# A two-layer decoder trunk in float32: raw x through the first projections with the rms factor applied at evictions, the router by channel halves, angles later, a layer's first group by terms

## The chip, the core and the metric

The kernel is one program on one core of a Trainium2 chip. The metric is the time of one execution on the device in microseconds (us), lower is better; a kernel's time is the median of its runs.

Engines, as the profile names them: PE (TensorE: matmuls and transposes, PEld its weight loads), DVE (VectorE), ACT (ScalarE), POOL (GpSimd) and SP (SyncE, which here issues nearly all DMAs). Engines run on their own and meet at semaphores.

## The reference

```python
def rms_norm(x, g):
    return x * lax.rsqrt(jnp.mean(x * x, axis=-1, keepdims=True) + EPS) * g

for l in range(DEPTH):                        # 2 layers, x is (1, 256, 1024) f32
    h = rms_norm(x, norm_mix_g[l])
    proj = h @ w_in[l]                        # u va | q k v | index q, k, weights | conv b c x | 3 gates
    ya = gelu(u) * spatial(layer_norm(gelu(va)))         # causal 128x128 mix per channel group
    yb = attention(q, k, v) over the 64 best causal keys of a small indexer, partial rotary
    yc = cb * conv3(cc * cx)
    x = x + (sigmoid(g0) * (ya @ w_proj_a) + sigmoid(g1) * (yb @ w_proj_b) + sigmoid(g2) * (yc @ w_proj_c)) @ w_out
    h = rms_norm(x, norm_ffn_g[l])            # best of 4 groups, then the 2 best of its 8 experts
    x = x + sum over the 2 experts e of weight_e * (silu(h @ w_gate[e]) * (h @ w_up[e])) @ w_down[e]
return rms_norm(x, norm_final_g)
```

All data is float32, the 256 tokens are two tiles of 128 (index t), the 1024 channels eight chunks of 128.

## The kernel before, in words

Each engine has a program of its own, written out by hand; the order of an engine's work is the order of its lines, and every wait is a semaphore. For each of the two layers:

**Mixers.** The projections run as 9 groups of 512 columns (the first, G_QI, has 324), then 6 gates, 6 branch projections and 2 halves of w_out. Each needs weights in two parts: SP loads a raw 1 MB half into one of 6 ring slots (load_mix), ACT rounds it to a high part (`high`, L740), DVE subtracts to get the low part (`low`, L944), and PE multiplies high by high, high by low and low by high into PSUM (`product`, L1392, 48 or 96 matmuls a group). A unit is the two halves of one group: unit 0 is G_QI, 1 G_Q, 2 G_K, 3 G_V, 4 G_VA, 5 G_U, 6 G_CX, 7 G_CC, 8 G_CB. G_QI to G_VA put tokens on the partitions, G_U, G_CX, G_CC and G_CB channels. Results alternate between psA and psB; a group waits until the result two before it was evicted (by ACT, or by DVE for the conv groups). The activations are split likewise into hT_high and hT_low.

**The start of a layer** (mixing_norm, in three programs): the squares of x are summed (ACT L705, DVE L959), a square root on ACT (L745) with one Newton step on DVE gives rstd, x is scaled by it (ACT L709, DVE L968), PE transposes it (L1422), ACT scales by the gain and rounds to hT_high (L696), DVE makes hT_low (L977). Between them DVE copies the layer's parameters and makes G_QI's low parts. G_QI's matmuls take all three terms of a channel chunk before the next chunk. In layer 0 DVE first works out the rotary angles (L894 to L906) and ACT their sines, and x, positions and two small tables come on SP's queue ahead of the weights, the router's weights on ACT's.

**The key selection** (DVE, L1034 to L1041): for each of the two token tiles 4 score operations and 8 rounds of MAX8 and MATCH_REPLACE8. Behind the second stand the statistics of va (L1048), then the low parts of G_CX.

**Routing**: DVE adds the w_out result to x, PE transposes x with channels strided by 8, ACT and DVE scale it by the ffn gain into hT, PE makes 16 router products, then spins (`spin`, matmuls whose result nobody reads) until DVE has the expert choice (members); rank products, a selection matrix, and the first gather follow.

**Experts**: 16 pairs of experts, each with 12 slots of 1 MB through the whole ring of 20; the last pair stands in a loop that also takes overflow blocks. SP refills a slot once its stage of the pair has been used (pair_freed).

## Time and profile before

| | us |
|---|---|
| median of 3 runs (1438.97 to 1439.96) | 1439.09 |
| the profiled execution's own time | 1437.3 |
| its span | 1435.6 |
| PE busy | 1385.5 (97%) |
| DVE busy | 559.2 (39%) |
| ACT busy | 361.2 (25%) |
| DMA moved | 490.19 MB, mean 341 GB/s |

The span runs from the first to the last instruction of the profiled execution. Times inside it are counted from its start. Layer 0's mixers take some 250 us, its routing 15, its experts 445; layer 1 begins near 716 and has the same stages. The profile's mean granted TensorE clock is 0.992 of full speed (2.4 GHz).

### The profile page before, as it was taken

To read this page: it belongs to the slowest core of one execution; us is meant where nothing else is said; L and a number is where in the kernel's file an instruction comes from. 1 tells how busy PE (TensorE), PEld (TensorE's weight loads), DVE (VectorE), ACT (ScalarE), POOL (GpSimd) and SP (SyncE) were. 2 spreads that over 40 slices of the span, in tenths; PEclk is the share of its full clock that TensorE was granted. 3 is DMA by queue.
4 is the path that set the end of the run, shared out by engine and by line. 5 is a ranking of instruction groups with operands and counts; after the bars stand their busy time and mean duration, and the time that the engine had idled before them with its cause. 6 is when DMAs were issued, how large, how long until landed. Compare 5 with 4: busy or idle time off the path is not lost.

```text
span 1435.6 us, 17698 instructions
## 1 busy us (share of the span) xinstructions
PE 1385.5 (97%) x7295; PEld 833.4 (58%) x7295; DVE 559.2 (39%) x882; ACT 361.2 (25%) x532; POOL 6.3 (0%) x36
## 2 busy tenths in 40 slices
PE   5999999999999999999889999999999999999996
PEld 5899888644444444444378988885444444444442
DVE  6686655432221221221267757355222122122213
ACT  5554442311111111111155444422111111111111
POOL 0000000000000000000000000000000000000000
PEclk9999999999999999999989999999999999999999
DMA  8655767899999999999946457578999999999995
GB/s 282 195 189 177 252 203 278 347 422 421 421 421 421 421 420 421 421 422 421 405 138 220 153 200 265 204 317 346 422 421 420 420 421 422 421 421 421 420 421 226
DMA packets 101125, 490.19 MB, mean 341 GB/s; under 512 B 8717, under 2 KB 12085, under 8 KB 51893
## 3 DMA queue, kind: packets, MB, share of 16 engines
q1 hardware_dynamic: 99940, 488.72, 85.4%
q8 instruction: 58, 0.95, 0.3%
q10 hardware_dynamic: 1104, 0.34, 0.1%
q14 instruction: 23, 0.18, 0.0%
HBM read 487.98 MB, written 1.05 MB: 341 GB/s over the span
## 4 chain that ended last, share of the span: by engine, by line
PE 89%; DVE 7%; issue 2%; ACT 1%; DMA 0%; DVEq 0%; SPq 0%; ACTq 0%
PE psB L1644 31%; PE psC L1655 16%; PE psA L1392 13%; PE psB L1392 12%; PE psA L1633 8%; PE psA L1670 3%; PE psA L1671 2%; DVE parts L944 2%; PE psD L1697 1%; DVE score_work L1039 1%; DVE top L1038 1%; ACT parts L740 1%; PE psC L1608 1%; DVE score_work L1034 0%; DMA rows<-in_conv_w_dram 0%
## 5 line engine op out<-in xcount | busy, mean ns | idle before, releaser
L1644 PE MATMUL psB<-slot,uT 128*64 128x512 f32 x2048 | 458.8, 595 | 0.0
L1644 PEld LDWEIGHTS psB<-slot,uT 128*64 128x64 f32 x2048 | 141.2, 137 | 268.4 <-issue 265.6
L1655 PE MATMUL psC<-slot,ybT_plain 128*64 128x512 f32 x1024 | 227.2, 595 | 2.8 <-ACT ybT_plain L855 2.7
L944 DVE TENSOR_TENSOR parts<-slot,parts 128x2048 fp32r<-128x2048 f32 (+1 forms) x80 | 177.4, 2248 | 70.3 <-ACT parts L740 70.0
L740 ACT ACTIVATE parts<-slot 128x2048 fp32r<-128x2048 f32 (+1 forms) x80 | 147.9, 1879 | 92.8 <-PE psA L1392 50.1
L1655 PEld LDWEIGHTS psC<-slot,ybT_plain 128*64 128x64 f32 x1024 | 70.9, 137 | 135.1 <-issue 128.2
L1268 DVE TENSOR_TENSOR x<-x,psA 128x1024 f32<-128x1024 f32 x62 | 75.7, 1221 | 186.3 <-PE psA L1671 186.3
L1392 PE MATMUL psB<-parts,hT_parts 128*128 128x512 f32 x448 | 138.9, 391 | 0.2
L1633 PEld LDWEIGHTS psA<-sel_mem,xn 128*128 128x128 f32 x1024 | 119.2, 192 | 27.0 <-issue 25.7
L839 ACT ACTIVATE rel_parts<-psC 128x512 fp32r<-128x512 f32 x62 | 37.1, 598 | 385.5 <-PE psC L1655 259.3
L1633 PE MATMUL psA<-sel_mem,xn 128*128 128x128 f32 x1024 | 127.4, 278 | 2.5 <-DVE sel_mem L1227 2.5
L1259 DVE TENSOR_TENSOR rel_parts<-psC,rel_parts 128x512 fp32r<-128x512 f32 x62 | 42.6, 688 | 222.3 <-ACT rel_parts L839 222.3
L1392 PE MATMUL psA<-parts,hT_parts 128*128 128x512 f32 (+1 forms) x384 | 115.3, 383 | 1.9 <-DVE low_mem_parts L977 1.9
L1392 PEld LDWEIGHTS psB<-parts,hT_parts 128*128 128x128 f32 x448 | 83.4, 188 | 18.5 <-DVE tmp L1151 1.0
L1280 DVE SCALAR_TENSOR_TENSOR ybT_plain<-score_work,slot_w,psB 128x512 f32<-128x512 f32 x32 | 23.9, 747 | 170.1 <-PE psB L1644 170.1
L1392 PE MATMUL psB<-parts,low_mem_parts 128*128 128x512 f32 x224 | 87.2, 389 | 0.0
L1392 PEld LDWEIGHTS psA<-parts,hT_parts 128*128 128x128 f32 x384 | 71.9, 192 | 14.8 <-issue 2.7
L1253 DVE TENSOR_TENSOR uT<-psA,g_ffn 128x512 f32<-128x512 f32 x64 | 44.3, 692 | 87.1 <-PE psA L1633 87.1
L1392 PE MATMUL psA<-parts,low_mem_parts 128*128 128x512 f32 (+1 forms) x192 | 73.1, 381 | 0.0
L855 ACT ACTIVATE ybT_plain<-psD 128x512 f32<-128x512 f32 x32 | 19.1, 597 | 165.6 <-PE psD L1697 165.6
L1670 PE MATMUL psA<-rel_parts,selT 128*128 128x512 f32 x124 | 55.5, 447 | 2.8 <-DVE rel_parts L1259 2.8
L1670 PEld LDWEIGHTS psA<-rel_parts,selT 128*128 128x128 f32 x124 | 23.2, 187 | 55.9 <-issue 48.7
(302 smaller groups left out, 1179.2 us busy)
## 6 DMA issues: line engine op xcount, KB each, us to landing
slot<-in_expert_w_gate_dram SPq DMA_DIRECT2D x128, 1024.0 KB, 21.7
slot<-in_expert_w_up_dram SPq DMA_DIRECT2D x128, 1024.0 KB, 23.2
slot<-in_expert_w_down_dram SPq DMA_DIRECT2D x128, 1024.0 KB, 24.3
slot<-in_w_in_dram SPq DMA_DIRECT2D x56, 1024.0 KB, 5.1
slot<-in_w_out_dram SPq DMA_DIRECT2D x8, 1024.0 KB, 5.1
slot<-in_w_proj_b_dram SPq DMA_DIRECT2D x4, 1024.0 KB, 5.0
slot<-in_w_proj_c_dram SPq DMA_DIRECT2D x4, 1024.0 KB, 4.9
slot<-in_w_proj_a_dram SPq DMA_DIRECT2D x4, 1024.0 KB, 5.0
```

Source lines behind the costliest of these rows:

```text
L740: sc.activation(high_and_low(i)[0], mix_slot(i), ACT.Copy).then_inc(high_act, 1)
L839: sc.activation(to[:, 0, :], psC[:, n, :], ACT.Copy).then_inc(y_act, 1)
L944: v.tensor_tensor(low_part, mix_slot(i), high_part, ALU.subtract).then_inc(low_dve, 1)
L1253: v.tensor_tensor(xT[:, 4 * b:4 * b + 4, :], psA[:, b, :].rearrange("p (c n) -> p c n", c=4), g_ffn[:, 4 * b:4 * b + 4].unsqueeze(2).to_br ...
L1259: v.tensor_tensor(to[:, 1, :], psC[:, n, :], to[:, 0, :], ALU.subtract).then_inc(y_dve, 1)
L1268: v.tensor_tensor(to, to, (psB if last and n else psA)[:, :, :], ALU.add).then_inc(x_added, 1)
L1392: ins = te.matmul(o, first, second, start=start and i == 0, stop=stop and i == len(TERMS) - 1)
L1633: ins = te.matmul(psA[:, b, (c % 4) * P:(c % 4 + 1) * P], xn[:, o:o + P], sel_plain[:, t, :], start=t == 0, stop=t == NT - 1)
L1644: ins = te.matmul(psB[j * BLK:(j + 1) * BLK, o, :], xT[:, 4 * half + c, j * BLK:(j + 1) * BLK], w[:, c, :], start=half == 0 and c == 0, st ...
L1655: ins = te.matmul(psC[j * BLK:(j + 1) * BLK, n, :], hidT[:, 2 * k + c, j * BLK:(j + 1) * BLK], w[:, c, n * 512:(n + 1) * 512], start=k == ...
L1670: te.matmul(ps[:, t, :], selT[:, t, :], y[:, 0, :], start=True, stop=False)
L1671: ins = te.matmul(ps[:, t, :], selT[:, t, :], y[:, 1, :], start=False, stop=True)
```

## The change

- **Raw x.** PE transposes x as it is, without rstd; ACT and DVE make hT_high and hT_low with the gain alone. rstd (now rstd_mix) is worked out behind them and applied where results are evicted: token-major groups and gates by ACT's scale, one instruction for each token tile (`normed`); for G_U and G_CX DVE multiplies by a row of rstd that PE makes with a ones matrix (`rstd_to_row`), for G_CX the row is squared, which covers the product with G_CC; G_CB's factor goes into its gate's product on DVE. G_U is therefore evicted by DVE, and ACT applies the gelu behind it.
- **The first group by terms.** In each half of G_QI all high by high products come first, then high by low weights, then low activations by high weights, each with its own wait; the high and low parts are made in that order.
- **Angles and sines** move behind the high and low parts of units 0 and 1. The small tables and positions go to ACT's queue, the router's loads to SP's, behind the sixth weight load; the router's weights are now laid out by chunks, so that they come in pieces of 16 and 128 bytes. Nine matmuls on ones open PE's program.
- **The router by channel halves.** x's channels are transposed without a stride; the first half of them between the two token tiles of the last w_out product; x is added by token tile. The ffn gain is multiplied into the router's weights, in `parameters`, which moves behind the low parts of unit 4. Each token tile's logits have their own signal. 15 spins instead of 14, and 4 more behind the rank products.
- **The key selection.** The low parts of G_CX are made between rounds 5 and 6 of the second selection; the statistics of va move behind the softmax's last step.

Three places, as the two kernels order them. ACT at the start of the program, before (parts are the high parts of a raw slot):

```order
L682 ACT_TABLE_LOAD
L682 ACTIVATE sin<-ang 128x32 [waits setup_link]
L683 ACTIVATE cos<-ang 128x32
L687 ACT_TABLE_LOAD
L687 ACTIVATE spare<-ones 128x1
L705 ACTIVATE xn,ss<-x 128x1024 [waits x_added,x_landed]
L745 ACTIVATE rstd<-inv 128x2 [waits inv_dve]
L740 ACTIVATE parts_81<-slot_75 128x1296 [waits staged2]
L709 ACTIVATE xn<-x,rstd 128x1024 [waits rstd_dve]
```

and in the change:

```order
L759 ACT_TABLE_LOAD [waits staged2]
L759 ACTIVATE parts_82<-slot_76 128x1296 [waits setup_done]
L703 ACTIVATE hT_parts<-psC,cols 128x256 [waits hT_ps]
...
L759 ACTIVATE parts_84<-slot_78 128x2048 [waits staged4]
L759 ACTIVATE parts_85<-slot_79 128x2048 [waits staged5]
L720 ACT_TABLE_LOAD
L720 ACTIVATE sin<-ang 128x32 [waits setup_link]
L721 ACTIVATE cos<-ang 128x32
L694 ACT_TABLE_LOAD
L694 ACTIVATE spare<-ones 128x1
L725 ACTIVATE xn,ss<-x 128x1024 [waits x_added,x_landed]
```

The weights' high parts and hT_high now stand ahead of the sines and the squares, and the program's first table load stands behind the wait for the first weights.

DVE in the second key selection, in the change:

```order
L1073 MAX top<-score_work 128x8 [waits dve_link]
L1074 MATCH_REPLACE score_work<-top,score_work 128x256 [waits dve_link]
L974 TENSOR_TENSOR parts_88<-slot_76,parts_82 128x2048 [waits dve_link,high_act]
L974 TENSOR_TENSOR parts_89<-slot_77,parts_83 128x2048 [waits high_act]
L1073 MAX top<-score_work 128x8
L1074 MATCH_REPLACE score_work<-top,score_work 128x256 [waits dve_link]
...
L1077 TENSOR_TENSOR maskb<-score_work 128x256 [waits dve_link]
L1078 SCALAR_TENSOR_TENSOR maskb<-maskb,causal 128x256 [waits dve_link]
L1084 TENSOR_TENSOR uT<-psB,rstd_row 128x1024 [waits mixed,dve_link]
```

The two low parts of G_CX stood behind the masks and four instructions of statistics; now three rounds and the masks stand behind them, and DVE's own eviction of G_U.

PE in the routing, in the change, from the last products of w_out on:

```order
L1463 MATMUL psD<-ident,x 128x128 [waits x_mixed]
L1463 MATMUL psD<-ident,x 128x128 x3
L1469 MATMUL psB<-r_w,hT 128x36 [waits routeT_act,layer_params]
L1469 MATMUL psB<-r_w,hT 128x36 x3
L1469 MATMUL psB<-r_w,hT 128x36 [waits routeT_act]
L1469 MATMUL psB<-r_w,hT 128x36 x3
L1463 MATMUL psD<-ident,x 128x128 [waits dve_out]
L1463 MATMUL psD<-ident,x 128x128
L1463 MATMUL psC<-ident,x 128x128 x2
L1469 MATMUL psB<-r_w,hT 128x36 [waits routeT_act]
```

Before, all 16 transposes stood behind the last add to x and ahead of all router products; now eight stand inside the w_out product, four behind its first token tile (x_mixed) and four behind the last add (dve_out).

The diff, cut to its core:

```diff
 sync_program:
-            with nc.allow_non_contiguous_dma(reason="256 positions"):
-                sp.dma_start(pos_i[:, :], positions.rearrange("a (t p) -> p (a t)", p=P)).then_inc(pos_landed, 16)
             for t in range(NT):
                 sp.dma_start(x[:, t, :], x_in[0, t * P:(t + 1) * P, :]).then_inc(x_landed, 16)
-            sp.dma_start(rows[0:DEPTH * KC, :], norm_mix_g.rearrange("l (c p) -> (l c) p", p=P)).then_inc(rows_landed, 16)
-            sp.dma_start(rows[DEPTH * KC:, :], conv_w.rearrange("l k (c p) -> (l k c) p", p=P)).then_inc(rows_landed, 16)
...
                     load_mix(i)
+                    if l == 0 and i == RAWS - 1:
+                        router_loads(sp)
...
-        def router_loads(act):
+        def router_loads(sp):
...
+                for l in range(DEPTH):
+                    sp.dma_start(rg_all[:, l], router_group_w.rearrange("l (c p) n -> l p c n", p=P)[l]).then_inc(router_landed, 16)
+                    sp.dma_start(re_all[:, l], router_expert_w.rearrange("l (c p) n -> l p c n", p=P)[l]).then_inc(router_landed, 16)
...
 scalar_program:
-            router_loads(act)
-            act.wait_ge(setup_link, TRIG_READY)
-
-            sc.activation(sin[:, :, :], ang[:, 0], ACT.Sin)
-            sc.activation(cos[:, :, :], ang[:, 1], ACT.Sin).then_inc(trig_act, 1)
+            act.dma_start(rows[0:DEPTH * KC, :], norm_mix_g.rearrange("l (c p) -> (l c) p", p=P)).then_inc(rows_landed, 16)
...
                 def mixing_norm():
 
+                    if l:
+                        act.wait_ge(pair_freed, start * STAGES)
+                    act.wait_ge(setup_done, 1)
+                    for i in range(2):
+                        high(unit_slots(0)[i])
+                        for b in (2 * i, 2 * i + 1):
+                            act.wait_ge(hT_ps, l * 4 + b + 1)
+                            even_bank((psC, psD)[i], b, hT_high, cols[:, l * KC:(l + 1) * KC])
+                    high(*unit_slots(1))
+                    if l == 0:
+                        act.wait_ge(setup_link, TRIG_READY)
+                        sc.activation(sin[:, :, :], ang[:, 0], ACT.Sin)
+                        sc.activation(cos[:, :, :], ang[:, 1], ACT.Sin).then_inc(trig_act, 1)
                     sqrt_table()
...
                     root_of(0)
-                    high(unit_slots(0)[0])
-                    act.wait_ge(rstd_dve, l * 2 + 1)
-                    sc.activation(xn[:, 0:D], x[:, 0, :], ACT.Copy, scale=rstd[:, 0:1]).then_inc(xn_act, 1)
-                    high(unit_slots(0)[1])
...
+                def normed(dst, n, func):
+
+                    ps = result(n)
+                    for t in range(NT):
+                        ins = sc.activation(dst[:, t, :], ps[:, t, :], func, scale=rstd_mix[:, t:t + 1])
+                    ins.then_inc(act_out, 1)
...
 vector_program:
                 def mixing_norm():
 
-                    squares(0)
-                    newton_step(l * 3 + 1, link).then_inc(rstd_dve, 1)
-                    dve.wait_ge(rstd_dve, l * 2 + 1)
-                    v.tensor_scalar(xn[:, D:2 * D], x[:, 1, :], rstd[:, 1:2], None, ALU.mult).then_inc(xn_dve, 1)
-                    parameters()
-                    dve.wait_ge(layer_params, l + 1)
-                    low(*unit_slots(0))
-
                     for b in range(4):
-                        dve.wait_ge(hT_act, l * 6 + b + 1)
+                        if b % 2 == 0:
+                            low(unit_slots(0)[b // 2])
+                        dve.wait_ge(hT_act, l * 4 + b + 1)
...
                     low(*unit_slots(1))
+                    if l == 0:
+                        angles()
+                    squares(0)
+                    newton_step(l * 3 + 1, link, rstd_mix).then_inc(rstd_dve, 1)
...
+                        if b == 1 and r == TOPK // 8 - 4:
+                            low(*unit_slots(6))
...
+                row = rstd_row[:, :].unsqueeze(1).unsqueeze(1).to_broadcast([P, 2, 2, S])
+                v.tensor_tensor(uT[:, :, :].rearrange("p (b h) s -> p b h s", b=2),
+                                result(G_U)[:, :, :].rearrange("p b (h s) -> p b h s", h=2), row, ALU.mult).then_inc(dve_out, 1)
...
 tensor_program:
+            pe.wait_ge(ones_set, 1)
+            for _ in range(9):
+                te.matmul(psC[:, 0, 0:P], ones[:, :], ones[:, :], start=True, stop=True)
...
+                    if step == G_QI:
+                        for i in range(2):
+                            use = USE[step, i]
+                            w = [part.rearrange("p (c n) -> p c n", c=4) for part in high_and_low(use)]
+                            for a, b in TERMS:
+                                for c in range(4):
+                                    k = 4 * i + c
...
+                            if part == 1 and t == 0:
+                                ins.then_inc(out_ps, 1)
+                                if half == 1:
+                                    pe.wait_ge(dve_out, l * len(on_dve) + 1 + on_dve.index(RESULT[out_of(0)]))
+                                    for u in range(NT):
+                                        route_transposes(psC[:, u, :], range(4), u)
...
+                route(1, 0).then_inc(route_ps, 1)
...
+                route(1, 1).then_inc(route_ps, 1)
+                spin(15)
```

## Rows read from the trace of the kernel before

**Rows 1.** waits of PE: waited for, us in total, times, longest us

```profile
PE psA L1392 <- DVE parts L944: 4.9, 2, 2.4
```

**Rows 2.** PE in order of time, start of layer 1: start, us, what [idle before]

```profile
721.57 1.97 PE L1422 MATMUL psA<-ident,xn 128*128 128x128 f32 x8 [5.64 <-ACT xn L709]
```

**Rows 3.** the chain that ended last: a layer's first and third group

```profile
37.28 10.93 PE psA L1392 x48
...
726.23 9.43 PE psA L1392 x48
...
747.24 10.93 PE psA L1392 x48
```

**Rows 4.** DVE and ACT in order of time, start of layer 1

```profile
717.43 1.22 DVE L959 CUSTOM_DVE_ANT_0 xn<-x 128x1024 f32<-128x1024 f32 x1
...
721.58 2.93 DVE L944 TENSOR_TENSOR parts<-slot,parts 128x1296 fp32r<-128x1296 f32 x2
...
724.43 1.65 DVE L977 SCALAR_TENSOR_TENSOR low_mem_parts<-psA,g_mix,hT_parts 128x256 fp32r<-128x256 f32 x4
...
719.21 1.27 ACT L740 ACTIVATE parts<-slot 128x1296 fp32r<-128x1296 f32 x1
...
722.78 1.63 ACT L696 ACTIVATE hT_parts<-psA,g_mix 128x256 fp32r<-128x256 f32 x4
...
726.01 3.71 ACT L740 ACTIVATE parts<-slot 128x2048 fp32r<-128x2048 f32 x2
```

**Rows 5.** DMAs of the start, us to landing; the first w_in load's; an SP issue

```profile
rg_all<-in_router_group_w_dram ACTq DMA_DIRECT2D x1, 32.0 KB, 4.0
...
g_ffn_all<-in_norm_ffn_g_dram ACTq DMA_DIRECT2D x1, 8.0 KB, 2.6
...
DMA to landing us min/median/max: 7.5/7.5/7.5
...
2.72 0.49 SPq L498 DMA_DIRECT2D rows<-in_conv_w_dram  x1
```

**Rows 6.** all engines in order of time, start of the program

```profile
3.75 0.17 DVE L894 CAST pos_f<-pos_i 128x2 f32<-128x2 int32 x1 [2.69 <-POOL causal L667]
...
6.49 1.28 ACT L687 ACT_TABLE_LOAD   x1
...
7.78 0.20 ACT L687 ACTIVATE spare<-ones 128x1 f32<-128x1 f32 x1
```

**Rows 7.** DVE, and PE's one wait, at the second key selection of layer 0

```profile
79.03 0.43 DVE L1038 MAX8 top<-score_work 128x8 f32<-128x256 f32 x1
...
83.46 1.29 DVE L1048 BATCH_NORM_STATS2 stats<-vg 128x6 f32<-128x512 f32 x2
...
85.47 4.47 DVE L944 TENSOR_TENSOR parts<-slot,parts 128x2048 fp32r<-128x2048 f32 x2
...
90.09 0.48 PE L1392 MATMUL psA<-hT_parts,parts 128*128 128x256 f32 x2 [2.44 <-DVE parts L944]
...
94.02 4.48 DVE L944 TENSOR_TENSOR parts<-slot,parts 128x2048 fp32r<-128x2048 f32 x2
```

**Rows 8.** PE and DVE, routing of layer 0

```profile
254.34 1.16 PE L1422 MATMUL psA<-ident,x 128*128 128x128 f32 x8 [1.31 <-DVE x L1172]
...
259.89 4.95 PE L1407 MATMUL psD<-before,ones 128*128 128x128 f32 x28
...
264.43 0.23 DVE L1212 TENSOR_TENSOR ycT_parts<-ycT 128x64 fp32r<-128x64 f32 x1
```

**Rows 9.** one stretch: busy us of each engine, granted clock, DMA share, GB/s

```profile
721.50:726.20 4.70, 3.68 (x16) 3.28 (x17) 4.67 (x8) 4.58 (x11) 0.00 (x0) 0.50 0.02 7
```

**Rows 10.** layer 0: two stretches; landing of the down parts issued at 677.4 and 679.5

```profile
270.00:274.20 4.20, 4.20 (x23) 1.67 (x23) 0.69 (x1) 0.00 (x0) 0.00 (x0) 1.00 0.03 14
...
290.00:600.00 310.00, 310.00 (x1588) 138.87 (x1586) 73.81 (x112) 38.65 (x99) 0.00 (x0) 1.00 1.01 421
...
DMA to landing us min/median/max: 28.6/28.8/29.1
```

More of the change, by code:

```diff
@@ L457, in build_trunk @@
         final_done = sem("final_done")
-        on_act = [n for n, step in enumerate(STEPS) if n <= G_U or is_gate(step)]
+        on_act = [n for n, step in enumerate(STEPS) if n < G_U or is_gate(step)]
         on_dve = [n for n in range(N_RESULTS) if n not in on_act]
@@ L766, in scalar_program @@
                 high(*unit_slots(3))
-                sc.activation(k_tok, result(G_K)[:, :, :], ACT.Copy).then_inc(act_out, 1)
+                normed(k_tok, G_K, ACT.Copy)
                 high(unit_slots(4)[0])
@@ L918, in variance, with newton_step @@
                 v.reciprocal(inv[:, :], var[:, :]).then_inc(inv_dve, 1)
-            def newton_step(n, step):
+            def newton_step(n, step, result=rstd):
                 dve.wait_ge(root, n)
@@ L1407, in spin, with route_transposes, route, norm_transposes @@
                         te.matmul(psD[:, 1, 0:P], ones[:, :], before[:, :], start=True, stop=True)
-                def norm_transposes(which):
-                    if which == 0:
-                        pe.wait_ge(xn_act, l * 2 + 1)
-                        pe.wait_ge(xn_dve, l + 1)
-                    else:
-                        pe.wait_ge(dve_out, (l + 1) * len(on_dve))
+                def route_transposes(bank, cs, t):
+                    for k, c in enumerate(cs):
+                        ins = te.transpose(bank[:, k * P:(k + 1) * P], x[:, t, c * P:(c + 1) * P], ident[:, :])
+                    ins.then_inc(routeT_ps, 1)
+                def route(half, t):
+                    for c in range(4 * half, 4 * half + 4):
+                        ins = te.matmul(psB[:, t, 0:N_ROUTE], hT[:, c, t * P:(t + 1) * P], r_w[:, c, :],
+                                        start=c == 0, stop=c == KC - 1)
+                    return ins
+                def norm_transposes():
+                    pe.wait_ge(x_landed, 16 * NT)
+                    pe.wait_ge(x_added, done * 2 + 1)
                     for b in range(4):
-                        ps = (psA, psB)[b // 2]
+                        ps = (psC, psD)[b // 2]
+                        if l == 0 and b == 3:
+                            pe.wait_ge(setup_done, 1)
                         for c in range(2):
@@ L1434, in group @@
                                 k = 4 * i + c
-                                if step == G_QI and k in (0, 4, 6):
-                                    pe.wait_ge(hT_dve, l * 6 + max(k // 2, 1) + 1)
                                 for t in range(NT):
@@ L1455, in index_transposes, with rstd_to_row @@
                     ins.then_inc(idxT_ps, 1)
+                def rstd_to_row():
+                    pe.wait_ge(diag_dve, l + 1)
+                    for t in range(NT):
+                        ins = te.matmul(psD[:, 1, t * P:(t + 1) * P], ones[:, :], rstd_diag[:, t, :], start=True, stop=True)
+                    ins.then_inc(row_ps, 1)
                 def index_scores():
                     pe.wait_ge(idxT_act, l + 1)
+                    pe.wait_ge(row_dve, l * 2 + 1)
                     for b, ps, nk in ((0, psD, P), (1, psC, S)):
```

237 lines of the change are left out of this document (140 added, 97 removed).

## The prediction

> **What bounds the kernel now.** I read the waits first, then the chain that ended last, then the timelines where they point. PE is busy for 97% of the span. Nearly all is matmul that the change leaves as it is, so only PE's gaps and its slow stretches can be won. Four kinds of gap are on the chain in each layer.
>
> - The start of a layer: PE sits idle for 5.64 us before its first transpose of layer 1 [rows 2], because x is summed, rooted and scaled first; G_QI starts at 726.23 and G_K at 747.24, in layer 0 G_K at 37.28 [rows 3]. PE pays twice: in 721.5 to 726.2 the granted clock is 0.50, the lower level of 1.2 GHz, after that idle time [rows 9], and G_QI takes 9.43 us.
> - Before G_CX PE waits 2.4 us for DVE's low parts, once a layer, 4.9 in all [rows 1, 7].
> - Routing: a wait of 1.31 us for x, then 16 transposes and 16 products up to 259.89, then spins that end at 264.84, as the choice does at 264.66 [rows 8].
> - The experts: DMA share 1.01 at 421 GB/s from 290 to 600, and 0.03 in 270 to 274.2, when the ring is full [rows 10]. From the first freed slot on the queue never rests, and the last down part, issued at 679.5, lands 29.1 us later, at 708.6. PE waits for no landing there, but uses this one at once: transfers and matmuls take the same 434 us. Both start with the first freed slot, so an earlier start moves both, and nothing is won or lost inside. I cost the experts and the end of the program at zero.
>
> **The change, part by part.** I measure the start of a layer at G_K's end: 48.2 and 758.2 before, both a start plus 10.93 [rows 3].
>
> *Layer 1.* x is complete at 717.43, where DVE's squares began [rows 4]. G_QI's first high part no longer waits for rstd and is made before that. Four transposes take 0.5, ACT's hT_high 0.82 a bank (1.63 for two) [rows 4]: G_QI starts at 718.8. ACT goes on: second bank 719.6, G_QI's second high part (1.27) 720.9, two banks 722.6, G_Q's two (3.71) 724.4 and 726.3 [rows 4]. DVE follows with low parts of 1.46 (2.93 for two) and 1.65 for two banks [rows 4], and 2.24 for a full one (4.48 for two) [rows 7]: G_Q's first is ready at 726.7. G_QI by terms has then run its 48 matmuls. At the full clock G_Q takes 10.9, to 737.6; the new row of rstd 0.5 and the index transposes 0.7 bring G_K's start to 738.8. Beside this stand squares, root and Newton step: DVE's low parts end at 729.0, squares 1.2 [rows 4]. Root and Newton are bounded by the 2.9 us between the end of the squares and the low parts at 721.58 [rows 4], which held more; I take 1.5. rstd is there at 731.7, G_QI evicted at 732.7, G_K's weights split in time (736.9). Nothing there is last. G_K ends at 749.7: **8.5 us** earlier.
>
> *Layer 0.* An SP issue takes 0.49 and three fewer stand ahead of the weights; the first load landed 7.5 us after its issue at 3.26 [rows 5], so now near 9.3. ACT's first table load, 1.28 [rows 6], stands behind that wait, so it is no longer hidden: 10.6. Then as above: two banks 13.5, second high part 14.8, two banks 16.4, G_Q's high parts 18.3 and 20.1, its low parts 20.5 and 22.8. G_Q runs to 31.4. Behind the low parts come the angles and sines, 2.7 (3.75 to 6.49) [rows 6], another table load 1.3, ACT's squares 1.1, root and Newton 1.5: rstd at 29.6, G_QI evicted 30.6, G_K's high part 32.5, its low part 34.7. Here the engines behind rstd are last, not PE. G_K ends at 45.6: **2.6 us** earlier. If the load comes no sooner the gain is 1.1; if the table load is hidden after all, 3.9.
>
> After each table load the next ACT operation follows at once (6.49 + 1.28, then 7.78) [rows 6], so I use 1.28. The Trainium skill (ScalarE: Activation LUTs, What ACT_TABLE_LOAD costs) puts a drain of about 1.38 us on top of each switch. By it the two loads on layer 0's path would cost 2.8 us more; the trace disagrees.
>
> *Before G_CX.* Its low parts move ahead of three rounds and the masks, 4.4 us (79.03 to 83.46), and of the statistics, 2.0 (to 85.47) [rows 7]. `parameters` moves in ahead of them at 0.9. They end 5.5 us sooner, 2.4 were needed: the wait goes, **2.4 us in each layer**. Late next would be G_CC's low parts. They ended at 98.5 [rows 7]; DVE loses the statistics there (2.0) and gains `parameters`, G_U's eviction (1.25, as other PSUM operations of this size) and the row's square (0.35), so 99.0 in the old frame. G_CX would now end at 87.7 + 11.7 = 99.4. The cover is 0.4 us.
>
> *Routing.* Behind w_out's end stood 1.31 + 5.55 us up to the last product [rows 8]. Now eight transposes (1.0) lie inside w_out, and eight more and the 16 products (4.5) need no wait for the first half of x: 5.5, so 1.3 sooner, and 1.6 for the choice because one tile's logits are handled early. But 15 spins at the old mean (4.95 for 14) [rows 8] take 5.3 and end 0.9 us behind the choice. Between 0.6 (spins last) and 1.6 (full clock) I take **1.0 in each layer**. The four spins behind the rank products fit into PE's wait for the selection matrix.
>
> *Free.* Evictions in two instructions, DVE's product with rstd for one gate, ACT's gelu behind DVE: ACT is busy 25% and DVE 39% of the span, and each has microseconds before its reader. The nine first matmuls run while x is on its way.
>
> Sum: 8.5 + 2.6 + 4.8 + 2.0 = 17.9 us. The profiled execution took 1437.3, so 1419.4 for such a run; it stood 1.8 below the median of 1439.1, so the median comes to **1421.2**.
>
> **The rivals.**
>
> *The wait moves to G_CC.* The cover of 0.4 rests on estimates of 2.5 us of added DVE work. If that comes to 2.4 us more, the gain before G_CX is given back before G_CC: 1426.0. For it: DVE has no gap in this stretch. Against: the statistics are gone. 0.12.
>
> *The clock stays low in layer 1.* PE still idles 1.5 us before the transposes and the last matmuls of a layer have gaps. With a granted 0.50, transposes take 1.9 and G_QI 2.1 more, G_Q starts some 3.6 later: 1424.8. Against: the idle time that went before the fall was 5.64 [rows 2, 9]. 0.13.
>
> *Small pieces stop SP's queue: slower.* The router's loads, some 4600 pieces of 16 to 128 bytes, now stand in SP's queue between G_K's and G_V's weights. The near rows: 256 pieces of 32 bytes landed in 2.6 us, 256 of 128 bytes in 4.0, issued 0.55 later [rows 5], so at most 1.95 for 256, and at 421 GB/s their bytes alone need 1.4 us in all. That is 1.4 to 35 us; I take 1 us for 256, 18 us. G_K's weights land near 22, G_V's then near 43 and 45, just in time for PE near 47. At 35 us PE loses 17: 1438. Above 2 us for 256 the change is slower; at 2.5, 1448. No row has pieces of 16 bytes. The Trainium skill (DMA: Bandwidth & Descriptors, Specifications) has every piece under 512 bytes pay a read-modify-write; by it this rival would come true if that doubled the rows' price. 0.08, of which 0.04 slower and 0.02 same.
>
> **The numbers.** 0.67 is left for the forecast. About 0.2% is what a measurement of this kernel can tell, 2.9 us. Faster by more 0.94, within 0.02, slower 0.04. The median forecast is 1421.2; the low end 1416.0 takes layer 0's upper bound and both full routings; the high end 1427.0 takes in the first two rivals. Beyond it lie both together and the third.
>
> **What would show it.** G_K ends near 45.6 in layer 0, and in layer 1 8.5 us nearer to the layer's last scatter; the granted clock is 1.00 in G_QI of layer 1; PE's wait for L944's successor before G_CX is gone and none stands before G_CC; the weights of G_V land before 45; the stretch from w_out's end to the gather is 2 us shorter (1.0 of it inside w_out); the DMA's busy stretch in the experts is 434 us as before. A stall on a landing in the first 60 us, or experts that stretch, would prove me wrong.

## The result and the profile after

The changed kernel takes 1418.70 us (median of 4 runs, 1418.14 to 1420.04) against 1439.15 beside it: a ratio of 0.9856, 95% interval 0.9841 to 0.9871, 20.45 us less. The forecast was 1421.2, with 17.9 us of gain. The profiled executions lie 17.3 us apart (spans 1435.6 and 1418.3). Executions of one kernel come at levels some 1.6 to 2 us apart; where two of them were traced, the difference was a short stretch at TensorE's lower clock. So places within the traces are compared here, and times only where they say enough. How far apart the medians lie depends on these levels too: beside the later experiments the kernel before had medians of 1437.48 (19 runs), 1439.18 (14, one of 5010.6 left out) and 1437.64 (7), and against 1437.6 the gain is 18.9 us.

PE is busy for 1386.7 us (98%), DVE 562.7, ACT 366.6. PE's waits, view of the waits of PE (waited for, us in total, times, longest), in answer to [rows 1]:

```profile
PE psA L1508 <- ACT hT_parts L703: 2.1, 1, 2.1
PE psD L1714 <- DVE ycT_parts L1261: 2.0, 2, 1.1
...
PE psC L1484 <- DVE x L1317: 1.5, 1, 1.5
...
PE psA L1443 <- DVE parts L974: 1.0, 1, 1.0
PE psB L1443 <- DVE tmp L1195: 0.5, 2, 0.3
PE psB L1443 <- DVE parts L974: 0.3, 2, 0.2
```

The 4.9 us before G_CX are gone. Twice 0.2 before G_CC, 2.0 before the rank products (L1714) and 0.3 in each layer at a gate product (L1195) are new. The chain that ended last, in answer to [rows 3] (the x96 rows are G_CC):

```profile
33.35 11.17 PE psA L1443 x48
...
95.61 11.75 PE psB L1443 x96
...
712.21 7.13 PE psA L1508 x48
719.34 11.14 PE psB L1443 x48
731.57 10.95 PE psA L1443 x48
...
793.58 11.74 PE psB L1443 x96
```

G_K of layer 0 ends at 44.5 (48.2 before). The start of layer 1, PE and then DVE in order of time, in answer to [rows 2, 4]:

```profile
710.24 1.09 PE L1484 MATMUL psC<-ident,x 128*128 128x128 f32 x8 [1.53 <-DVE x L1317]
711.17 1.04 PE L1484 MATMUL psD<-ident,x 128*128 128x128 f32 x8
711.96 2.65 PE L1508 MATMUL psA<-parts,hT_parts 128*128 128x324 f32 x16
```

```profile
710.22 1.51 DVE L974 TENSOR_TENSOR parts<-slot,parts 128x1296 fp32r<-128x1296 f32 x1
...
716.98 4.49 DVE L974 TENSOR_TENSOR parts<-slot,parts 128x2048 fp32r<-128x2048 f32 x2 [0.19 <-ACT parts L759]
...
723.88 0.16 DVE L956 TENSOR_TENSOR rstd_mix<-rstd,newton 128x2 f32<-128x2 f32 x1
```

x is complete at 710.19, PE multiplies from 711.96 on, and rstd, ready 13.9 us after x, is late for nothing. Two stretches of the changed kernel (busy us of each engine, granted clock, DMA share, GB/s), in answer to [rows 9]:

```profile
712.20:719.30 7.10, 7.10 (x49) 6.85 (x47) 6.67 (x11) 7.08 (x9) 0.00 (x0) 1.00 0.49 157
...
956.00:963.10 7.10, 5.95 (x39) 5.63 (x39) 2.62 (x11) 0.00 (x0) 0.00 (x0) 0.76 0.81 338
```

G_QI of layer 1 has the full clock. Layer 1's first gather has not: 5.46 us where layer 0's took 3.81. So this execution lost 1.6 us that executions with a fast gather do not lose.

The account of the profiled pair, each line the shift between the two traces:

| stretch | layer 0 | layer 1 |
|---|---|---|
| start of the layer to G_K's end | 3.7 | 8.4 |
| G_K's end to G_CC's start | 2.5 | 2.5 |
| G_CC to the last group ahead of the routing | -0.4 | -0.4 |
| from there to the gather | 1.1 | 1.1 |
| the gather at the lower clock | | -1.6 |
| gather to the end of the layer | 0.3 | 0.05 |

The sum is 17.3 (the entries are rounded). Without the slow gather it is 18.9.

### The profile page after: what moved, and what is told of

The parts are those of the page before. It is cut to its first block, busy times and chain, and to the rows that moved or that the text cites. A ratio compares the mean times of both kernels' runs of the same rounds, so it can differ in the third digit from the quotient of the medians.

```text
span 1418.3 us, 17835 instructions
## 1 busy us (share of the span) xinstructions
PE 1386.7 (98%) x7341; PEld 835.1 (59%) x7341; DVE 562.7 (40%) x892; ACT 366.6 (26%) x555; POOL 6.3 (0%) x36
## 4 chain that ended last, share of the span: by engine, by line
PE 87%; DVE 8%; ACT 3%; issue 2%; DMA 0%; DVEq 0%; SPq 0%; ACTq 0%
PE psB L1743 32%; PE psC L1754 16%; PE psB L1443 12%; PE psA L1443 10%; PE psA L1732 9%; PE psA L1769 3%; DVE parts L974 3%; PE psA L1770 2%; PE psD L1796 1%; DVE score_work L1074 1%; DVE top L1073 1%; ACT parts L759 1%; ACT xn L749 1%; PE psA L1508 1%; DVE score_work L1069 0%
## 5 line engine op out<-in xcount | busy, mean ns | idle before, releaser
L1443 PE MATMUL psA<-parts,hT_parts 128*128 128x512 f32 x320 | 99.3, 391 | 1.0 <-DVE parts L974 1.0
L1443 PEld LDWEIGHTS psA<-parts,hT_parts 128*128 128x128 f32 x320 | 59.5, 188 | 13.2 <-issue 1.2
L1443 PE MATMUL psA<-parts,low_mem_parts 128*128 128x512 f32 x160 | 62.3, 390 | 0.0
```

The lines of the kernel that those rows point to most:

```text
L1443: ins = te.matmul(o, first, second, start=start and i == 0, stop=stop and i == len(TERMS) - 1)
```

## Experiments

### The kernel before once more

> The kernel before, unchanged, profiled in every run. The two profiled executions compared so far lie 17.3 us apart, the medians 20.5. In the changed kernel's profiled execution the gather behind layer 1's routing ran at a granted clock of 0.76 and took 5.46 us where layer 0's took 3.81; its other runs were some 1.5 us shorter. Theory: the kernel before has the same kind of step in its ordinary runs, so here spans should come in two or three levels some 1.6 us apart, with a granted clock that differs in a short stretch around a gather, and the medians' 20.5 is 18.9 of schedule and 1.6 of clock. Rival: the profiled execution of before (1437.3) was simply short everywhere; then the levels are not 1.6 apart and no stretch differs in clock.

Ten runs: 1436.95 to 1441.63, median 1440.22, ratio 1.0011 (1.0 to 1.0023), at levels near 1437, 1439.2 and 1441.3. The traced one took 1439.08; what makes the third level no trace shows. The difference from the first trace of before lies in one place, the chain's first row:

```profile
18.30 9.43 PE psA L1392 x48
...
39.32 10.91 PE psA L1392 x48
```

G_QI of layer 0 took 9.43 us here and 7.33 in the first trace; everything behind it is 1.7 to 2.0 later, up to the end. The first gathers were alike (3.81 and 3.84), so the place that I named was wrong and the kind right. The row of the stretches reads a granted clock of 1.00 in it, though each matmul takes as long as in layer 1 at the lower level:

```profile
18.30:27.70 9.40, 9.40 (x49) 9.40 (x50) 5.91 (x6) 3.51 (x2) 0.00 (x0) 1.00 0.72 251
```

Three of the four traces of before or of its variants have 9.3 to 9.4 there. The first trace of before was thus short beside the four runs whose median is 1439.15, the one of the changed kernel long beside its own. From 17.3, with 1.7 to 2.0 for G_QI and 1.6 for the gather, come 20.6 to 20.9; the medians say 20.45. This fits, but it is not more than that: of 54 runs of the kernel before (these ten, the four of the result and the 40 above) 23 took less than 1438 us, so neither form of G_QI is the rule, and only one trace is of such a run.

### The clock at the start of layer 1

```diff
                     if which == 0:
+                        if l:
+                            for _ in range(42):
+                                te.matmul(psC[:, 0, 0:P], ones[:, :], before[:, :], start=True, stop=True)
                         pe.wait_ge(xn_act, l * 2 + 1)
```

This is a variant of the kernel before.

> The kernel before with 42 matmuls on constants that fill PE's idle time ahead of layer 1's first transposes; nobody reads them. Theory (the slow stretch at the start of layer 1 is the clock after PE's idle time): granted clock 1.00 in the transposes and in G_QI, the transposes take about 2.0 for 16 where they took 3.7, G_QI 7.3 to 7.5 where it took 9.43, and G_K ends 3 to 3.6 us nearer to the last scatter; total 1435.5 to 1436.2 against 1439.1. So of the 8.4 us that layer 1's start gained, some 3.3 would be clock and 5.1 the idle time and the order of the work. Rival: the clock is not set by that idle time, G_QI stays at 9.4 and the total within 0.5 us.

Median 1439.35 of 10 (1436.52 to 1440.7), ratio 1.0003 (0.9992 to 1.0014): the 1435.5 to 1436.2 that I expected did not come. The 42 took 9.38 us, not the 5.3 that I had in mind, since each is two matmuls in the records. G_QI had the full clock, but began 2.3 us late:

```profile
717.96 9.38 PE psC L1414 x84
730.54 7.33 PE psA L1392 x48
```

> The kernel before with 22 matmuls on constants in PE's idle time ahead of layer 1's first transposes: 42 of them took 9.38 us in the run before, longer than the idle time of 5.6, and put G_QI at the full clock (7.33 us) but 2.3 us late, so that G_K began at the same place. 22 take 4.9 us and end before the transposes' input is there. Theory (clock after idle time is a part of layer 1's gain): transposes 2.0 for 16, G_QI 7.3 to 7.5, G_K ends 3 to 3.6 us nearer to the last scatter than in the kernel before (there 40.7 us from x complete to G_K's end). Rival: 4.9 us of such matmuls are not enough to keep the clock, and G_QI stays above 9.

With 22 of them the median is 1438.22 of 10 (1437.07 to 1444.39), ratio 1.0 (0.9987 to 1.0012). PE in order of time, and the stretch of G_QI:

```profile
723.30 1.09 PE L1425 MATMUL psA<-ident,xn 128*128 128x128 f32 x8 [0.73 <-ACT xn L709]
...
727.96 0.53 PE L1392 MATMUL psA<-parts,hT_parts 128*128 128x324 f32 x2 [2.69 <-DVE low_mem_parts L977]
```

```profile
728.00:736.80 8.80, 8.80 (x49) 8.80 (x50) 5.78 (x6) 2.94 (x2) 0.00 (x0) 0.81 0.28 85
```

The transposes were fast, but G_QI began no earlier: it waits for DVE's low parts, for 2.69 us where the wait was 0.98, and in the middle of G_QI the clock fell again (8.89 us). From the last scatter to G_K's end it took 43.8 us for 44.4, so 0.5 was won and not 3. Matmuls in the idle time alone win next to nothing in the kernel before: DVE's low parts are last there. Of layer 1's 8.4 us the lower clock holds the 2.3 of G_QI (9.43 to 7.13), which the changed kernel has because PE starts G_QI early and runs through it. 6.8 are the start of G_QI (by the chain 2.0 behind x instead of 8.8), and 0.65 goes the other way between G_Q and G_K, where the new row of rstd stands. No run puts the scaling of x back by itself, so that the 6.8 come from raw x is read from the two traces.

### The two moves in the key selection, undone one at a time

```diff
-                        if b == 1 and r == TOPK // 8 - 4:
-                            low(*unit_slots(6))
...
+                low(*unit_slots(6))
                 row = rstd_row[:, :].unsqueeze(1).unsqueeze(1).to_broadcast([P, 2, 2, S])
```

> The changed kernel with the low parts of G_CX back behind the masks of the second selection (the statistics of va stay late). Theory (DVE's position of these two instructions was the whole wait before G_CX): the low parts end near 85.2 in layer 0 where they ended at 80.9, PE waits 1.3 to 1.5 us before G_CX in each layer (2.4 less the 1.1 that the late statistics and the order still give), DVE's total in this stretch is unchanged so G_CC's low parts end at the same distance, and G_CC begins 1.2 to 1.5 later in each layer: total plus 2.4 to 3.0 against the changed kernel's 1418.7. Rival (DVE is the bound of the whole stretch, PE's waits only move): PE's wait before G_CX comes back and G_CC's start does not move, total within 0.5.

Median 1423.89 (1422.99 to 1424.51), ratio 0.9897 (0.9878 to 0.9916): 5.2 us above the changed kernel, where 2.4 to 3.0 were expected. PE waits before G_CX in both layers:

```profile
87.13 0.47 PE L1442 MATMUL psA<-hT_parts,parts 128*128 128x256 f32 x2 [1.50 <-DVE parts L974]
...
788.14 0.47 PE L1442 MATMUL psA<-hT_parts,parts 128*128 128x256 f32 x2 [1.52 <-DVE parts L974]
```

G_CC begins 52.66 and 52.65 us behind G_K's end, for 51.09 and 51.06 in the changed kernel: 1.6 in each layer, 3.2 in all. The profiled executions lie 4.4 apart: these 3.2, 1.7 for G_K of layer 0 at the lower clock (12.79 for 11.17), which the edit, made 40 us later, cannot have caused, less 0.5 because G_CC, with no wait ahead of it, takes 11.52 again. One gather was slow in each. So the move is worth 3.2 us by the places; what else is in the medians' 5.2 no second trace shows.

The statistics alone:

```diff
+                dve.wait_ge(act_out, l * len(on_act) + 1 + on_act.index(G_VA))
+                for t in range(NT):
+                    ins = v.bn_stats(stats[:, t, :], vg[:, t, :])
...
+                variance(mv[:, :, 1], 1.0, link)
                 row = rstd_row[:, :].unsqueeze(1).unsqueeze(1).to_broadcast([P, 2, 2, S])
```

> The changed kernel with the statistics of va back ahead of G_U's eviction, the low parts of G_CX left early. Theory (cover before G_CC is nearly nothing: PE waited 0.3 us in all for these low parts in the changed kernel): the four instructions take 2.0 us, G_CC's low parts end 2.0 later and PE waits 1.9 to 2.1 before G_CC in each layer: total plus 3.8 to 4.2 against 1418.7, which would show that the rival of the prediction in which the wait moves to G_CC was one step away. Rival: G_CC's start has slack that the chain does not show; total plus 0 to 1.

Median 1423.09 (1422.33 to 1424.15), ratio 0.9891 (0.9873 to 0.991). PE now waits before G_CC, and in layer 0 the clock fell behind that wait:

```profile
97.83 0.47 PE L1443 MATMUL psB<-hT_parts,parts 128*128 128x256 f32 x2 [2.18 <-DVE parts L974]
...
799.53 0.47 PE L1443 MATMUL psB<-hT_parts,parts 128*128 128x256 f32 x2 [2.16 <-DVE parts L974]
```

```profile
97.80:111.10 13.30, 13.27 (x98) 13.30 (x99) 9.18 (x13) 3.14 (x3) 0.00 (x0) 0.87 0.38 145
```

G_CC begins 53.08 and 53.05 behind G_K's end, plus 1.99 in each, 4.0 in all; the median rose by 4.4. G_CC of layer 0 took 13.24 for 11.75, about what the changed kernel's trace lost at its slow gather. So the wait before G_CX goes with one move and would have come back before G_CC without the other. There is no cover: PE waits 0.2 before G_CC in the changed kernel.

### Layer 0: the table load

```diff
+            act.wait_ge(ones_set, 1)
+            sc.activation(spare2[:, :], ones[:, 0:1], ACT.Copy)
```

> The changed kernel with one small activation on constants at the start of ACT's program, so that the first table load does not stand behind the wait for the first weights. Theory (layer 0's start is one chain from the first weights' landing through ACT and DVE, and the table load is on it as forecast): the first high part begins at 7.9 where it began at 9.20, and everything up to G_K's start follows 1.28 earlier, G_K ends at 43.2; total minus 1.3. Rival (the transposes of x, ending at 9.2, or DVE's queue take over at once): G_K ends within 0.4 us of 44.5.

Median 1418.89 (1418.69 to 1421.03), ratio 0.9858 (0.9842 to 0.9873): the median shows no gain. ACT, PE, and the stretch of G_K:

```profile
8.41 1.28 ACT L763 ACTIVATE parts<-slot 128x1296 fp32r<-128x1296 f32 x1 [4.18 <-DMA slot<-in_w_in_dram]
```

```profile
32.56 0.70 PE L1447 MATMUL psA<-parts,hT_parts 128*128 128x512 f32 x2 [1.85 <-DVE parts L978]
```

```profile
32.50:39.00 6.50, 6.44 (x21) 5.17 (x22) 6.43 (x10) 4.89 (x5) 0.00 (x0) 0.74 0.75 275
```

The load, now at 2.73, is off the chain as expected. The first high part began at 8.41, since the weights landed 0.5 later in this execution, and G_K 0.79 earlier: ACT's and DVE's chain passes the shift on whole. But PE stood 1.85 us before G_K instead of 1.01, and G_K took 12.78 instead of 11.17. It ended at 45.3, 0.8 later than in the changed kernel.

The edit is not the cause of that. The experiment with the low parts (a_low6), with its table load in the old place, has the same wait and the same slow G_K:

```profile
19.01 0.73 PE L1442 MATMUL psB<-parts,hT_parts 128*128 128x512 f32 x2 [0.18 <-DVE parts L974]
...
33.42 0.70 PE L1442 MATMUL psA<-parts,hT_parts 128*128 128x512 f32 x2 [1.85 <-DVE parts L974]
```

The first of these lines is G_Q's start. What tells the executions apart is G_QI of layer 0. In three traces (a_table, a_low6 and the Exp experiment below) it took 7.4 us, G_Q ended early, and PE waited 1.85 us for DVE's low part; G_K then took 12.8. In the six others of the changed kernel and its single edits G_QI took 8.8 to 9.4, the wait was 0.4 to 1.0 and G_K took 11.1 to 11.2. So where ACT and DVE are late, a fast G_QI makes PE wait longer, and the execution is slower for it. Against the two traces of its own kind, whose G_K ends at 46.2 and 46.3, a_table ends 0.9 and 1.0 earlier: the table load was on the path, as the first theory had it.

### Routing: the Exp table, the spins

```diff
+                    sc.activation(spare[:, :], ones[:, 0:1], ACT.Exp)
                     act.wait_ge(rstd_dve, l * 2 + 2)
```

> The changed kernel with a small Exp on constants ahead of ACT's wait for the second rstd, so that the table load of 1.28 us that now stands between ACT's scaling of x and the exponential falls into ACT's idle time. In the changed kernel DVE waits 0.76 and 0.87 us for that exponential behind the choice, in the kernel before not at all. Theory: this is why the choice came 1.8 us sooner behind w_out but the gather only 0.9; the waits go and the gather begins 0.7 to 0.9 earlier behind w_out's end in each layer, total minus 1.6. Rival (as the forecast had it, PE's spins end last): they end at 255.8, before the choice; then nothing changes in the gather's start.

ACT and DVE in the changed kernel, which this run takes aside:

```profile
251.85 4.20 ACT L749 ACTIVATE xn<-x,rstd 128x1024 f32<-128x1024 f32 x2 [0.86 <-DVE rstd L956]
256.07 1.28 ACT L862 ACT_TABLE_LOAD   x1
257.36 0.21 ACT L862 ACTIVATE ex<-ex 128x10 f32<-128x10 f32 x1
```

```profile
257.61 0.16 DVE L1264 TENSOR_REDUCE gsum<-ex 128x2 f32<-128x8 f32 x1 [0.76 <-ACT ex L862]
```

With the table loaded early, median 1418.11 (1416.95 to 1418.67), ratio 0.985 (0.9834 to 0.9866). The gather of layer 0, in the changed kernel and then in this one:

```profile
259.75 3.81 PE L1732 MATMUL psA<-sel_mem,xn 128*128 128x128 f32 x32 [1.14 <-DVE sel_mem L1276]
```

```profile
260.68 3.81 PE L1733 MATMUL psA<-sel_mem,xn 128*128 128x128 f32 x32 [0.29 <-DVE sel_mem L1277]
```

From the rank products to the gather it is now 2.01 us for 2.85, in layer 1 1.98 for 2.87: 0.84 and 0.89 won, as the first theory had it. The medians show 0.6 of these 1.7, which is within the spread of the runs; the profiled execution had the fast G_QI and with it G_K of layer 0 at the lower clock (12.76).

```diff
-                spin(4)
```

> The changed kernel without the four spins behind the rank products. PE is then idle from the last rank product to the gather but for nothing: 2.3 us in one piece behind 1.1 before the choice. In the traces so far the gather ran at the full clock (3.81 us for 32) or, in some executions of each kernel, at a lower one (5.46), with the four spins in place. Theory: the idle time ahead decides how often; without the spins both gathers are slow in most runs, total plus 1.6 to 3.2. Rival: the spins do nothing, gathers and total as before within the spread of 1.6.

Median 1422.76 (1422.16 to 1423.27), ratio 0.9894 (0.9877 to 0.991). Both gathers are slow:

```profile
259.76 5.44 PE L1731 MATMUL psA<-sel_mem,xn 128*128 128x128 f32 x32 [2.12 <-DVE sel_mem L1276]
...
959.37 5.47 PE L1731 MATMUL psA<-sel_mem,xn 128*128 128x128 f32 x32 [2.14 <-DVE sel_mem L1276]
```

The four spins are worth 1.6 us in each layer whose gather they keep fast. The median rose by 4.1; two slow gathers are 3.3 of it, and the rest no trace shows.

```diff
-                spin(15)
+                spin(24)
...
-                spin(4)
+                spin(7)
```

> The changed kernel with 24 spins ahead of the choice instead of 15 and 7 behind the rank products instead of 4, which fills PE's idle time of 1.08 and 1.14 us on either side. Spins are 0.24 us each at the full clock: they end at 256.9 with the choice at 256.85, and at 259.4 with the selection matrix at 259.6. Theory: no idle time ahead of the gather, so it runs at the full clock in every execution; total 1418.1 to 1418.9 with a spread under 1 us. Rival: the lower clock has another reason than idle time; gathers of 5.4 us still turn up, and totals 1.6 apart.

Median 1419.59 (1418.19 to 1420.58), ratio 0.9867 (0.9851 to 0.9884). Both gathers ran at the full clock (3.77 and 3.74), and yet the spread is 2.4. In layer 1 the clock was low in the spins themselves, with PE busy all the way, and they ended 2.1 us behind the choice:

```profile
951.20:953.00 1.80, 1.80 (x10) 1.80 (x10) 1.24 (x10) 1.80 (x2) 0.00 (x0) 0.50 1.01 419
```

```profile
951.04 6.85 PE L1458 MATMUL psD<-before,ones 128*128 128x128 f32 x48
```

The same stretch of layer 1 was slow with 15 spins too, in the experiments on the order of terms and on the loads below (5.05 and 5.20 us for the 30 records that took 3.59 elsewhere). There they ended 0.5 and 0.7 us behind the choice and moved the gather by 0.1 to 0.2. So idle time is one reason for a lower clock and not the only one, and more spins than fit are a risk.

### The order of terms, and the router's loads

```diff
-                            for a, b in TERMS:
-                                for c in range(4):
+                            for c in range(4):
+                                for a, b in TERMS:
```

> The changed kernel with G_QI's matmuls in the old order, all three terms of a chunk before the next, so that its first matmuls wait for low parts. Theory (by terms first is worth the low parts' time): in layer 1 G_QI starts at 712.6 for 712.0 (first weights' low part ready at 711.7, hT_low's first bank later), its second half has to wait for the second low part at 715.2 and hT_low to 716.8, and ends at 720.5 to 721 where it ended at 719.3: G_K ends 1.2 to 1.6 later; layer 0, whose start is bound by ACT and DVE up to G_K, within 0.3. Total plus 1.2 to 1.9. Rival: with raw x and early high parts the old order would have done as well, plus 0 to 0.5.

Median 1420.17 (1418.73 to 1421.54), ratio 0.9878 (0.9861 to 0.9894). By the chain PE's order is worth nothing:

```profile
712.24 7.30 PE psA L1508 x48
...
731.62 10.95 PE psA L1443 x48
```

From the first transpose of x to G_K it is 21.35 us, for 21.33 in the changed kernel. Each low part is there when the old order asks for it: the second weights' part is done at 715.3, and the second half begins at 715.8. I had the second half begin too early. Only PE's order was put back here: ACT and DVE still make the high and low parts in the new order. Layer 0's G_K starts at 33.40 for 33.35. The median rose by 1.5 us, as the first theory had it, but two of the four runs took the 1418.8 of the changed kernel and two 1421.5; why, no trace shows. The profiled one took 1418.73.

```diff
                     if l == 0 and i == RAWS - 1:
                         router_loads(sp)
...
+                sp.dma_start(ring_slots[0][:, 0:16].rearrange("p (l c) -> p l c", l=DEPTH), norm_ffn_g.rearrange("l (p c) -> p l c", c=KC)).then_inc(router_landed, 16)
...
-                    dve.wait_ge(router_landed, 16 * (3 + 2 * DEPTH))
+                    dve.wait_ge(router_landed, 32 * (3 + 2 * DEPTH))
```

> The changed kernel with the router's seven loads issued twice on SP's queue, the second copy into an unused ring slot, both waited for. In the changed kernel the seven issues hold SP's queue from 9.30 to 23.77, 14.5 us, and G_V's weights, issued then, land before 35 while PE asks for them near 46. Theory (the price of the small pieces is SP's issue time and it is hidden): twice 14.5 us put G_V's first issue at 38.2; its parts land near 44 and 46 at ACT, which needs them with 4.2 us of high and low part before PE: G_V starts 2 to 4 us late, total plus 2 to 5. So one set of loads is free with some 10 us to spare. Rival (the forecast's rate of 1 us for 256 pieces, 18 us a set): G_V's weights land 18 us later than that, near 62, total plus 16 to 20.

Median 1418.70 (1418.45 to 1420.91), ratio 0.9869 (0.9852 to 0.9885): nothing at all. SP's queue, the first set and the second:

```profile
10.70 3.39 SPq L643 DMA_DIRECT2D rg_all<-in_router_group_w_dram  x1
14.13 4.09 SPq L644 DMA_DIRECT2D re_all<-in_router_expert_w_dram  x1
18.27 2.99 SPq L643 DMA_DIRECT2D rg_all<-in_router_group_w_dram  x1
...
24.97 0.58 SPq L652 DMA_DIRECT2D slot<-in_router_expert_w_dram  x1
...
28.56 23.57 SPq L514 DMA_DIRECT2D slot<-in_w_in_dram  x7
```

The second set takes 4.6 us where the first took 14, and within the first set the two equal issues of re_all took 4.09 and 0.59. So the long issues are not the price of the pieces; they stand close behind six weight loads, most likely waiting for these. Once they are through, an issue takes 0.4 to 0.9 us. ACT waited 1.1 and 0.8 us for G_V's weights and PE for nothing: G_V starts at 46.00 for 45.95. Both theories overpriced the loads, mine by taking the 14.5 us of the first set for a price.

### Both small activations, and another order in layer 0

The changed kernel with the two small activations, and in layer 0:

```diff
 scalar_program, mixing_norm:
-                    if l == 0:
-                        act.wait_ge(setup_link, TRIG_READY)
-                        sc.activation(sin[:, :, :], ang[:, 0], ACT.Sin)
-                        sc.activation(cos[:, :, :], ang[:, 1], ACT.Sin).then_inc(trig_act, 1)
                     sqrt_table()
...
-                high(*unit_slots(2))
+                high(unit_slots(2)[0])
+                if l == 0:
+                    act.wait_ge(setup_link, TRIG_READY)
+                    sc.activation(sin[:, :, :], ang[:, 0], ACT.Sin)
+                    sc.activation(cos[:, :, :], ang[:, 1], ACT.Sin).then_inc(trig_act, 1)
+                high(unit_slots(2)[1])
 vector_program:
-                    if l == 0:
-                        angles()
                     squares(0)
...
                     ins.then_inc(diag_dve, 1)
+                    if l == 0:
+                        angles()
...
+                if l == 0:
+                    low(unit_slots(2)[0])
                 dve.wait_ge(trig_act, 1)
...
-                low(*unit_slots(2))
+                low(*unit_slots(2)[0 if l else 1:])
```

> The changed kernel with both small activations (table load and Exp ahead), and in layer 0 with the squares, the root and rstd ahead of the angles and sines, the sines between G_K's two high parts. Theory: 1.28 at the start, 0.76 + 0.87 in the routing, and at most 1.0 more from the order (PE's wait before G_K goes, nothing behind it moves by more): G_K of layer 0 ends at 42.2 to 43.2, total minus 2.9 to minus 3.9 against the changed kernel, some 1415. Rival: DVE's low part of G_K's second half now comes behind the rotation and PE waits for it in the middle of G_K; then G_K takes longer than 11.2 and the order gives nothing.

Median 1414.58 of 5 (1413.57 to 1414.9), ratio 0.9826 (0.9812 to 0.984): 4.1 us below the changed kernel. Its chain:

```profile
10.93 8.01 PE psA L1516 x48
...
30.98 10.95 PE psA L1451 x48
```

G_K ends at 41.9, 2.6 earlier, without a wait ahead of it and at the full clock; the expectation was 42.2 to 43.2. With 0.84 and 0.89 in the routing that makes 4.3. The five runs lie within 1.3 us. How the 2.6 divide between the table load and the order this run does not show.

## Why the prediction was right, point by point

*Layer 1's start, 8.5 forecast, 8.4 measured.* The steps hold one by one: G_QI began 1.8 behind x complete (1.4 forecast), G_Q 9.1 (9.3), G_K 21.4 (21.4), rstd was there at 13.9 (14.3), and the clock stayed at 1.00. What I did not say is which part of the change did it. PE's order by terms, in which I put G_QI's early start, is worth nothing; raw x with the early high parts is enough. These two, and the new order of ACT and DVE, were not taken apart.

*Layer 0's start, 2.6 forecast, 3.7 measured in the pair.* The chain through ACT and DVE was last, as forecast, and the table load was on it (7.91 to 9.19). The term that was mis-sized is the landing of the first weights: I let it come 7.5 us after its issue, it came 6.1 after it, at 7.84 instead of 9.3. (My sum up to rstd is also 0.2 too long: its terms give 29.4 and not 29.6.) And against an execution of before whose G_QI takes 9.4 and not 7.33, the gain there is 5.3 to 5.7. In the changed kernel a slow G_QI costs nothing, because ACT and DVE are later, and a fast one costs: G_K then ends near 46.2 and not at 44.5. I had read G_QI of layer 0 from one trace and had not asked how often it takes 9.43, though layer 1 showed that value [rows 3].

*Before G_CX, 4.8 forecast, 5.1 measured at G_CC's start,* less 0.2 in each layer in G_CC itself and 0.2 behind it, so 4.3 in the end: G_CC takes 11.75 now for 11.52, with the wait of 0.2 ahead of it, and PE waits 0.27 for a gate product. In place of the forecast cover of 0.4 there is that wait of 0.2. That the wait moves to G_CC was the nearest rival, and the statistics put back made it true for 4.0 us. Its price was too high by its own figures: 2.4 us more behind a cover of 0.4 give back 4.0 and not 4.8.

*Routing, 2.0 forecast, 2.2 measured, for a wrong reason.* The step that failed is that 15 spins end 0.9 us behind the choice. In both layers of the profiled execution they ran at the full clock, 3.6 us for 15, and ended before it; where they were slow, in layer 1 of two experiments, they ended 0.5 and 0.7 behind it. Counted from the last group ahead of the routing, the choice came 2.0 us sooner in layer 0 and the gather 1.1; the other 0.85 was lost in a place I had not priced: the table load ahead of the exponential, whose slack in the kernel before was 0.6 us. ACT there in the kernel before:

```profile
262.06 1.28 ACT L835 ACT_TABLE_LOAD   x1
263.95 0.21 ACT L835 ACTIVATE ex<-ex 128x10 f32<-128x10 f32 x1 [0.61 <-DVE ex L1206]
```

I called ACT free by its busy share of 25%, and that was the mistake. The two errors, a choice that came sooner and a gather that did not follow, nearly cancel, so the right number here is luck.

*The sum and the step to the median.* Without the slow gather the terms measured 18.9 for 17.9 forecast: layer 0 gave 1.1 more, the stretch before G_CX 0.5 less, routing and experts 0.5 more together. I added 1.8 us to the profiled execution's time, as the measured distance of before. For the changed kernel the profiled execution was 1.3 above its median. The distance is not a property of the profile; it goes with where the lower clock falls. Of the 2.5 us by which the median lies below the forecast, 1.0 is in the terms and 1.5 in this step.

*The rivals.* The clock of layer 1 stayed high. G_V's weights were there in time; SP's queue cost nothing. (The bytes of the router's loads, 332 KB, need 0.8 us at 421 GB/s and not the 1.4 of the forecast; nothing hung on it.) The experts took 450.4 us from gather to x complete, for 450.7 before, as forecast.

## What to carry to other kernels

When an edit makes one engine's chain shorter, list what stands between its stages on the other engines with less than the gain as slack, table loads among them; a low busy share says nothing of that. An early start is worth more when it also removes a wait ahead of a long run of matmuls. A longer wait can cost more than its own length: behind 1.85 us G_K took 1.6 us more than behind 1.0. So a gain should be looked for in the order that keeps PE fed, and before one trace is held against another, the groups ahead of the edit should be seen to agree, or the difference is put down to the wrong cause. Before a duration goes into a sum, look at the same group in the other layer: where they differ, the group may have two durations in both layers.

## What the runs showed of the hardware

- A stretch at the lower clock costs 1.6 to 2 us when PE is on the path. In layer 0 G_K took 11.1 to 11.2 us behind an idle time of 0.4 to 1.0 (six traces) and 12.8 behind one of 1.85 (three traces). First gathers took 5.45 behind 2.1 (two of two), 3.8 behind 0.3 (four of four), and either behind 1.1. Behind 2.2 before G_CC one of two was slow, behind 2.4 before G_CX of the kernel before none.
- It also came with PE busy without a gap, in the spins of layer 1, in three traces of nine of the changed kernel and its single edits (clock 0.50 in 951.2 to 953 of the one with 24 spins). What set it off there is open.
- In the first 30 us the granted clock can read 1.00 while matmuls take the time of the lower level (9.43 us for G_QI, 7.33 in another execution of the same kernel). The duration is the surer sign.
- Of seven issues of loads with pieces of 16 to 128 bytes, three took 3.0 to 4.1 us each on SP's queue close behind six weight loads; the same seven again, later, took 0.4 to 0.9 each.
- A table load took 1.28 us wherever one was read here, and an activation that waits for nothing else follows at once, at 9.20 after 7.91. The drain of some 1.38 us that the Trainium skill (ScalarE: Activation LUTs, What ACT_TABLE_LOAD costs) adds was seen in none of these places.
